# Closing sums of both expert stages on TensorE in four PSUM banks, and 13 idle products around the first turning

## What is computed

```python
# every block ends like this (ALPHA = 4 ** 0.25)
x = layer_norm(ALPHA * x + mix, ln_mix_g[layer], ln_mix_b[layer])
ffn = expert_choice_moe(x, moe_w_router[layer], moe_w_gate_up[layer], moe_w_down[layer])
x = layer_norm(ALPHA * x + ffn, ln_ffn_g[layer], ln_ffn_b[layer])

# expert_choice_moe: each of 16 experts takes its 32 best tokens
out = einsum(silu(g) * u, w_down) * gates
return zeros_like(x).at[bi, idx].add(out)          # added back to the tokens

# layer_norm: y = (x - mean) * (var + eps) ** -0.5 * gain + bias, over 1024 features
```

## Time and profile before

| what | value |
|---|---|
| median of 3 runs | 1569.71 us (1567.81 to 1576.83) |
| the profiled execution: its own time | 1567.92 us |
| its span in the trace | 1566.6 us |
| mean granted TensorE clock | 0.883 of full speed |
| busy: TensorE, VectorE, ScalarE, GpSimd | 73%, 29%, 20%, 4% |
| read from HBM | 501 MB, 320 GB/s over the span |

### The profile page before, as it was taken

One profiled execution on the slowest core, in us unless ns is written; L12 is line 12 of the kernel. 1 busy time (PEld: TensorE's weight loads), 2 busy tenths in 40 slices (PEclk: granted clock), 3 DMA queues, 4 the chain that ended last, 5 costly groups with the idle time before them and its releaser, 6 DMA issues.

```text
span 1566.6 us, 18985 instructions
## 1 busy us (share of the span) xinstructions
PE 1140.2 (73%) x8361; PEld 635.7 (41%) x8361; DVE 447.2 (29%) x902; ACT 306.7 (20%) x596; POOL 67.9 (4%) x90
## 2 busy tenths in 40 slices
PE   7998655677475555998875555655555699989897
PEld 6746211244131111876541111111111188645893
DVE  4534202101120000756340100000010078555643
ACT  4421110001310000365110000000000047334320
POOL 2000100000000000012000000000000020000100
PEclk9999878899788887999997887787787799999999
DMA  9908999999999999633999999999999934205520
GB/s 297 360 1 322 422 425 424 427 414 420 424 425 427 424 425 414 207 100 138 401 421 424 427 424 426 427 425 424 427 426 423 403 138 144 105 14 190 178 80 27
DMA packets 89763, 503.33 MB, mean 321 GB/s; under 512 B 7011, under 2 KB 15665, under 8 KB 56913
## 3 DMA queue, kind: packets, MB, share of 16 engines
q1 hardware_dynamic: 84320, 492.78, 77.7%
q10 hardware_dynamic: 3680, 8.04, 1.5%
q0 software_dynamic: 1680, 1.30, 0.3%
HBM read 501.00 MB, written 1.10 MB: 320 GB/s over the span
## 4 chain that ended last, share of the span: by engine, by line
issue 29%; PE 28%; DMA 26%; DVE 9%; ACT 4%; POOL 1%; SPq 1%; DVEq 0%; ACTq 0%; POOLq 0%
DMA weight_ring<-in_moe_w_gate_up 11%; DMA weight_ring<-in_moe_w_down 10%; PE bank L423 3%; PE bank L324 3%; PE bank L325 3%; PE bank L326 3%; PE bank L1296 3%; DMA weight_spare<-in_ada_w 3%; DMA weight_ring<-in_even_w_in 2%; PE bank L436 2%; PE bank L1323 2%; DVE weight_ring_rounded L364 1%; PE bank L870 1%; PE bank L2326 1%; POOL norm_rstd L472 1%
## 5 line engine op out<-in xcount | busy, mean ns | idle before, releaser
L1296 PE MATMUL bank<-weight_ring,expert_tokens 128*32 128x512 f32 x2048 | 318.3, 757 | 208.8 <-DMA weight_ring<-in_moe_w_gate_up 203.0
L1296 PEld LDWEIGHTS bank<-weight_ring,expert_tokens 128*32 128x32 f32 x2048 | 66.8, 125 | 432.5 <-DMA weight_ring<-in_moe_w_gate_up 248.4
L1323 PE MATMUL bank<-weight_ring,actT 128*32 128x256 f32 x2048 | 167.6, 485 | 80.7 <-DMA weight_ring<-in_moe_w_down 71.4
L1323 PEld LDWEIGHTS bank<-weight_ring,actT 128*32 128x32 f32 x2048 | 76.9, 134 | 158.4 <-DMA weight_ring<-in_moe_w_down 70.7
L1417 DVE TENSOR_TENSOR act<-silu,bank 128x256 f32<-128x256 f32 x32 | 13.4, 420 | 438.9 <-ACT silu L1467 438.9
L1467 ACT ACTIVATE silu<-bank 128x256 f32<-128x256 f32 x32 | 12.3, 384 | 485.4 <-PE bank L1296 485.4
L1422 DVE COPY expert_outs<-bank 32x256 f32<-32x256 f32 x64 | 26.7, 418 | 270.4 <-PE bank L1323 269.4
L364 DVE TENSOR_TENSOR weight_ring_rounded<-weight_ring,weight_ring_rounded 128x1024 fp32r<-128x1024 f32 (+1 forms) x62 | 71.6, 1214 | 14.5 <-ACT weight_ring_rounded L348 14.5
L348 ACT CAST weight_ring_rounded<-weight_ring 128x1024 fp32r<-128x1024 f32 (+1 forms) x68 | 65.9, 1041 | 35.2 <-DMA weight_ring<-in_odd_w_in 13.2
L1476 ACT COPY expert_outs<-bank 32x256 f32<-32x256 f32 x64 | 23.3, 365 | 237.9 <-PE bank L1323 237.2
L472 POOL TENSOR_TENSOR norm_rstd<-norm_var,minus_half 128x1 f32<-128x1 f32 x12 | 18.3, 1527 | 949.7 <-DVE norm_var L460 949.7
(11 more groups left out here) (467 smaller groups left out, 1763.4 us busy)
## 6 DMA issues: line engine op xcount, KB each, us to landing
weight_ring<-in_moe_w_gate_up SPq DMA_DIRECT2D x128, 2048.0 KB, 31.2
weight_ring<-in_moe_w_down SPq DMA_DIRECT2D x64, 2048.0 KB, 31.1
weight_ring<-in_ada_w SPq DMA_DIRECT2D x8, 2048.0 KB, 17.3
weight_ring<-in_even_w_in SPq DMA_DIRECT2D x5, 2048.0 KB, 14.7
weight_ring<-in_odd_w_in SPq DMA_DIRECT2D x5, 2048.0 KB, 8.9
weight_spare<-in_ada_w SPq DMA_DIRECT2D x4, 2048.0 KB, 20.4
weight_ring<-in_lru_w_in SPq DMA_DIRECT2D x4, 2048.0 KB, 23.6
weight_ring<-in_attn_w_qkv SPq DMA_DIRECT2D x2, 2048.0 KB, 16.1
```

The lines of the kernel that those rows point to most:

```text
L1296: last = pe.matmul(up[CAP * j:CAP * (j + 1), :], B.xs[:, t, e * CAP:(e + 1) * CAP], w[:, t % 2, :, j, :], start=(t == 0), stop=(t == T - 1))
L1323: last = pe.matmul(K[3][CAP * q:CAP * (q + 1), 0:QC], B.actT[i][:, s, j * CAP:(j + 1) * CAP], w[:, jj, s, q, :], start=(j == 0 and s == 0) ...
```

## The change

TensorE now forms the closing sum. For the last expert of each stage it multiplies `x` by the identity into four banks (4, 0, 6, 7; one for each half and c), ahead of the down products, leaves the banks open, and adds the four products with `back` to them (`start=False`). VectorE no longer adds; `experts_norm_vector` reads mean, variance and the centred tokens out of the banks. In layer 0 ScalarE computes mean and variance of half 1 (`experts_moments_scalar`), in layer 1 VectorE does both halves. The 36 idle products behind the stage stay. At the very start 5 idle products stand ahead of the turning and 8 behind it, into bank 6.

```diff
@@ attention_tensor
         pe.wait_ge(*sig.after("ident"))
+        self.idle_products_tensor(K[6], 5)
         self.turn_x_tensor("attention", K)
+        self.idle_products_tensor(K[6], 8)
@@ experts_tensor, ahead of the down products
+            if e == NE - 1:
+                for half in range(H):
+                    for c in range(2):
+                        pe.wait_ge(*sig.after("summed", stage, half, c, grp - 1))
+                        pe.matmul(K[self.SUM_BANKS[2 * half + c]], B.ident, B.x[:, half, c * 512:(c + 1) * 512], start=True, stop=False)
@@ experts_tensor, behind them
                 pe.wait_ge(*sig.after("back", stage, grp // 2))
+                if e == NE - 1:
+                    for half in range(H):
+                        for c in range(2):
+                            pe.matmul(K[self.SUM_BANKS[2 * half + c]], B.back[:, grp, half * P:(half + 1) * P],
+                                      B.outs[grp % 2][:, c * 512:(c + 1) * 512], start=False, stop=True).then_inc(
+                                *sig.tell("experts_back", ("summed", stage, half, c)))
+                    break
+    SUM_BANKS = (4, 0, 6, 7)
@@ experts_vector
+                        if e == NE - 1:
+                            break
...
-                        if e == NE - 1:
-                            self.stats_vector(stage, half, c)
-                    if e == NE - 1:
-                        self.norm_vector(stage, half, EPS_FIRST)
+        self.experts_norm_vector(stage, layer)
+
+    def experts_norm_vector(self, stage, layer):
...
+        def moments(half):
+            for c in range(2):
+                v.wait_ge(*sig.after("summed", stage, half, c))
+                v.bn_stats(B.stats[:, half, 6 * c:6 * c + 6], K[self.SUM_BANKS[2 * half + c]]).then_inc(
+                    *sig.tell("moments", ("moments", stage, half, c)))
+            v.wait_ge(*sig.after("moments", stage, half, 1))
+            v.bn_aggr(B.mv[:, half, :], B.stats[:, half, :]).then_inc(*sig.tell("moments", ("mean", stage, half)))
+            v.wait_ge(*sig.after("mean", stage, half))
+            v.tensor_scalar(B.var[:, half:half + 1], B.mv[:, half, 1:2], EPS_FIRST, None, ALU.add).then_inc(
+                *sig.tell("variance", ("variance", stage, half)))
+
+        moments(0)
+        v.wait_ge(*sig.after("rows", stage))
+        for half in range(H):
+            if half:
+                v.wait_ge(*sig.after("variance", stage, 1))
+            for c in range(2):
+                cols = slice(c * 512, (c + 1) * 512)
+                v.scalar_tensor_tensor(B.x[:, half, cols], K[self.SUM_BANKS[2 * half + c]], B.mv[:, half, 0:1], B.gain[:, cols],
+                                       ALU.subtract, ALU.mult).then_inc(*sig.tell("moments", ("centred", stage, half)))
+            if half == 0 and layer == 1:
+                moments(1)
+            v.wait_ge(*sig.after("centred", stage, half))
+            v.wait_ge(*sig.after("deviation", stage, half))
+            x = B.x[:, half, :]
+            v.scalar_tensor_tensor(x, x, B.rstd[:, half:half + 1], B.bias, ALU.mult, ALU.add).then_inc(*sig.tell("normed", ("x", stage, half)))
+
+    def experts_moments_scalar(self, stage):
...
+        for c in range(2):
+            a.wait_ge(*sig.after("summed", stage, 1, c))
+            a.activation(B.junk[:, c, :], banks[c], ACT.Identity, accum_out=sums[:, c:c + 1]).then_inc(*sig.tell("bank_moments"))
...
+        for c in range(2):
+            a.activation(B.junk[:, c, :], banks[c], ACT.Square, bias=sums[:, 2:3], accum_out=sums[:, 3 + c:4 + c]).then_inc(
+                *sig.tell("bank_moments"))
...
@@ experts_scalar, last
+        if layer == 0:
+            self.experts_moments_scalar(stage)
```

More of the change, by code:

```diff
@@ L1432, in experts_vector @@
                         v.tensor_tensor(xsum, xsum, K[(4, 0)[c]], ALU.add).then_inc(
-                            *sig.tell("summed", ("summed", stage, half, c, grp), ("summed", stage, half, c)))
-                        if e == NE - 1:
-                            self.stats_vector(stage, half, c)
-                    if e == NE - 1:
-                        self.norm_vector(stage, half, EPS_FIRST)
+                            *sig.tell("summed", ("summed", stage, half, c, grp)))
+        self.experts_norm_vector(stage, layer)
@@ new lines, in experts_norm_vector @@
+    def experts_norm_vector(self, stage, layer):
+        sig, v, B, K = self.sig, self.v, self.B, self.B.bank
+        def moments(half):
[23 more added lines that the diff above has]
+            v.scalar_tensor_tensor(x, x, B.rstd[:, half:half + 1], B.bias, ALU.mult, ALU.add).then_inc(*sig.tell("normed", ("x", stage, half)))
@@ new lines, in experts_moments_scalar @@
+    def experts_moments_scalar(self, stage):
+        sig, a, B, K = self.sig, self.a, self.B, self.B.bank
+        banks = [K[b] for b in self.SUM_BANKS[2:4]]
+        sums, mean = B.sums, B.mv[:, 1, 0:1]
+        for c in range(2):
+            a.wait_ge(*sig.after("summed", stage, 1, c))
+            a.activation(B.junk[:, c, :], banks[c], ACT.Identity, accum_out=sums[:, c:c + 1]).then_inc(*sig.tell("bank_moments"))
+        a.wait_ge(*sig.now("bank_moments"))
+        a.activation(sums[:, 1:2], sums[:, 1:2], ACT.Identity, bias=sums[:, 0:1]).then_inc(*sig.tell("bank_moments"))
+        a.wait_ge(*sig.now("bank_moments"))
+        a.activation(sums[:, 2:3], sums[:, 1:2], ACT.Copy, scale=-1.0 / D).then_inc(*sig.tell("bank_moments"))
+        a.activation(mean, sums[:, 1:2], ACT.Copy, scale=1.0 / D).then_inc(*sig.tell("bank_moments", ("mean", stage, 1)))
+        a.wait_ge(*sig.now("bank_moments"))
+        for c in range(2):
+            a.activation(B.junk[:, c, :], banks[c], ACT.Square, bias=sums[:, 2:3], accum_out=sums[:, 3 + c:4 + c]).then_inc(
+                *sig.tell("bank_moments"))
+        a.wait_ge(*sig.now("bank_moments"))
+        a.activation(sums[:, 4:5], sums[:, 4:5], ACT.Identity, bias=sums[:, 3:4]).then_inc(*sig.tell("bank_moments"))
+        a.wait_ge(*sig.now("bank_moments"))
+        a.activation(B.var[:, 1:2], sums[:, 4:5], ACT.Copy, scale=1.0 / D, bias=EPS_FIRST).then_inc(
+            *sig.tell("bank_moments", ("variance", stage, 1)))
@@ L2719, in buffers @@
     B.stats, B.mv, B.var, B.rstd = M.take("norm_stats", H, 12), M.take("norm_mv", H, 2), M.take("norm_var", H), M.take("norm_rstd", H)
+    B.sums = M.take("bank_sums", 8)
     ring = M.at
@@ L2762, in buffers @@
     _, B.hot = M.take_both("hot", H, NE * CAP)
+    B.junk = M.place("sum_junk", M.at - 1024, [2, 512])
     B.xs = M.take("expert_tokens", T, NE * CAP)
```

## The result

The changed kernel takes 1563.3 us (median of 9 runs), the kernel before 1571.56 (9 runs beside them). One of the nine runs, 2651.05 us, was slow and is left out of the ratio; the other eight have the median 1562.6. The ratio is that of the means, **0.9936**, with a 95% interval of 0.9914 to 0.9957: 10 us less (7 to 14). The forecast was 1562.0 with a gain of 6.3.

A forecast was written before the change was run, and what follows sets the result against it. Bound: expert stages as long as their weight loads, so time saved at their start or ends should reach the program's end. From 1567.9 us, 2.4 + 0.5 + 1.8 + 1.6 = 6.3 gives 1561.6, stated as 1562.0; range 1558.5 to 1568.5.

The forecast's parts named there:

- Start, 2.4: Program start: 13 idle products raise TensorE's clock before the first projections, whose first twelve products take 2.8 us, not 5.24.
- so it moves along: Start: the copy of the first result at 25.77 follows TensorE at once, so it comes earlier with the projections.
- Layer 0, ahead of the down products, 0.5: End of layer 0's experts: four identity products keep TensorE busy, so the last down products end 0.5 us earlier.
- as there is no rest left in which it fell: Layer 0's second down batch: the clock stays high without the earlier rest, ending at 624.7 instead of 625.1.
- 617.24 to 620.9: Layer 0: the expected place of the four identity products, 0.91 us each and 3.6 together, ahead of the down products.
- Layer 0, behind them, 1.8: Layer 0, products with `back` to the turning: 11.8 us in place of 13.55, the idle products being the new bound.
- Layer 1, 1.6: End of layer 1's experts: GpSimd free 0.9 us earlier and its split quarter 0.7 shorter, so half 1 comes 1.6 earlier.
- (a): Start: the high clock is lost again or comes late; in the first form gain 0.8, total 1563.6. Chance 0.16.
- its second form: Start: the turning does not count as work, some four products stay slow, gain 1.2, total 1563.2.
- (b): The four sum products meet a low clock: layer 0's stage ends 1.3 us late, layer 1's slack absorbs it; 1563.8. Chance 0.17.
- (c): Slower: the clock stays low through the four products and both down batches, +8 us, nothing gained at start; 1577. Chance 0.05.
- (d): A gain does not arrive because a load or queue behind has its own time: 1563.5 to 1564.5, all lost 1568. Chance 0.10.

The follow-up runs named there:

- start_only: The kernel before plus only the 13 idle products at the start (5 ahead of the first turning, 8 behind it): 1570.13 us, ratio 0.9984.
- ends_only: The changed kernel without its 13 idle products at the start, so only the new ends of both expert stages: 1561.74 us, ratio 0.9930.
- idle_ahead_down: The kernel before plus 16 idle products ahead of the last expert's down products in each layer: 1570.75 us, ratio 0.9999.
- after_again: The changed kernel run once more, nothing changed: 1560.96 us, ratio 0.9927 against the kernel before.
- layer0_only: The changed kernel with its new end in layer 0 alone, no idle products at the start, layer 1 as before: 1566.21 us, ratio 0.9961.
- idle28: The changed kernel with 28 idle products in place of 36 behind layer 0: 1559.07 us, ratio 0.9921 against the kernel before.
- idle20: The changed kernel with 20 idle products in place of 36 behind layer 0: 1558.81 us, ratio 0.9928 against the kernel before.

## Why the prediction was right

**Start, 2.4.** Product 48 came 2.10 earlier in the pair of profiles, the late beginning of 0.24 among it, and start_only measured 2.5. The mechanism was right, but the twelve slow products were those of one profile: of the five other kernels without products behind the turning, four take 12.45 to 12.62 us where the profile of before has 13.40 (the fifth, ends_only, 13.62), so the usual gain is 1.5. Nor do the products always hold the clock, as start_only's profile shows. What lies between 1.5 and the 2.5 that start_only measured is within its interval. The step "so it moves along" holds only in part. The prediction took the start's gain to reach the end of layer 0's stage whole; but in all seven kernels with the thirteen products the last expert weights of layer 0 landed 5.8 to 6.6 us behind the ones before them, and in the other seven 5.0. By medians the last landing is 1.2 us earlier with the thirteen products, the one before it 2.15. Why the last load takes longer there, the traces do not tell; it is one reason why start and ends together bring less than their sum.

**Layer 0, ahead of the down products, 0.5.** 3.46 became 1.98, 1.5 us. The prediction's own times give 625.1 - 624.7 = 0.4, so this term was mis-sized by a factor of three. It rests on the step "as there is no rest left in which it fell"; but there was a rest, 1.37 us, and the clock did not fall in it. The step "617.24 to 620.9" put the four products 4.4 us ahead of the landing, as in an execution whose last gate and up products ran at the low clock (window 610 to 615 of the kernel before: 0.67); in the changed kernel they began 6.9 ahead. Slow gate and up products are only one part of that: idle_ahead_down has them, with as much work in that place, 4.4 ahead, and 3.05 us; but after_again has them too (3.62 us), its four products began 5.9 ahead since the landing was late, and it has 1.98. ends_only and layer0_only, whose last landing was not late, have 1.98 as well. Other profiles with old ends have 2.60 to 3.66, those with new ends 1.98 to 2.73: by their medians 1.3 us.

**Layer 0, behind them, 1.8.** 14.53 became 12.57, 2.0 earlier (1.8 predicted, though 13.55 - 11.84 is 1.7), and 12.57 stands in every profile with the new end in layer 0 and 36 idle products. That these would be the new bound was right, and idle28 gives the spare as 1.5 (1.4 predicted). ScalarE's chain took 628.56 - 621.44 = 7.1 us (7.5 predicted); the casts ended at 632.34, 0.7 ahead of the turning (0.4 predicted).

**Layer 1, 1.6.** From the load of `even_w_in` to the second turning, 12.48 became 10.79, 1.7 us, by the two steps named: GpSimd free at once, and its quarter at 2.08. Against the other profiles with old ends (11.45 to 13.57, median with it 11.8) it is 1.0.

**The sum.** 6.3 was forecast; 8.3 was measured by the medians and 10 by the ratio, whose interval of 7 to 14 lies above the forecast. That the time itself came so near, 1562.0 against 1563.3, is in part luck: the gain was put too small, and the kernel before, reckoned at 1567.9 to 1569.7, turned out at 1571.56. The ends carry the miss: 3.9 was forecast for them, and ends_only measured 11 (7 to 15). The terms as the profiles' medians have them are 1.5, 1.3, 2.0 and 1.0, or 5.8, of which the late last landing takes something back. Another 1.3 lies in the recurrent block (27.0 against 25.67, medians), where the low clock came in four of the six profiles with old ends in both layers and in one of seven with new; that the new ends cause this is not shown. The rest may be that the long low stretch of the even block is rarer behind the new ends: there it stood in four of five profiles of old ends in both layers with the wait left open, and in two of five of new. That is too few to call it shown, so about half of what ends_only measured is not placed. The prediction left out altogether that a run's total carries some 6 us from that one place.

**The rivals.** (a) came about in one profile of a kernel with thirteen products, in its first form; its second form is refuted. (b) came about in one of the seven profiles with the new end in layer 1, with all four products slow, and the slack took it up; in part it came about in layer 0 of idle28 and idle20. (c) rested on "a low stretch of some 10 us of unbroken work; the longest that I read is 5.24": there are stretches of 17 us of unbroken work in the even block, and with rests between the products there is one inside layer 0's expert stage in the very trace that was read (window, busy us with instructions, granted clock, DMA share, GB/s):

```profile
410.33:427.40 17.07, 5.03 (x46) 0.50 1.01 430
```

So the chance of 0.05 was given for a reason that does not hold, though (c) did not come about in any profile. (d) did not come about in the stages, where each gain is seen; of the start's gain a part is lost on the way to the end of layer 0's stage.

## What to carry to other kernels

Before a gain of some microseconds is read from two profiles, find out by how much executions of one kernel differ and where: here what followed one wait of 1.2 us in an untouched block moved the total by 6 us, and the kernel before with that wait filled measured 0.47% less where the whole change brought 0.64%. Products for nobody are worth most, in these profiles, right ahead of work that would otherwise begin after a rest; count them against the moment at which the real operand is ready, since one too many is a new bound. And price a step against the landing it waits for from more than one execution.

## What the runs showed of the hardware

- TensorE worked for 17 us (once for 20) all but without a pause at 1.2 GHz, after a wait of 1.17 us, in seven profiles of 11, and most of the same work ran at 2.4 GHz in others.
- GpSimd's power of one column takes 0.56 us beside VectorE's product from a bank (624.67) and 1.52 beside VectorE's product of two tensors of the state buffer (1250.29). The Trainium skill, SBUF — State Buffer, SBUF: two separate sides, says that a VectorE operation with two SBUF inputs holds a port pair that GpSimd needs; the trace agrees. So reading the sums from the banks speeds up GpSimd too, by 1 us; in layer 0 VectorE's wait for it (0.52 us at 638.18 in the earlier trace rows) is gone from the row at 630.04. The turning did not gain by it, as the idle products were the bound.
- It goes the other way too: VectorE's last operation of the norm took 3.05 us beside GpSimd's split of 2.09 in the earlier trace rows, and 1.28 in the earlier trace rows, without it.
